# Expert pairs of a hybrid decoder step: the pair's combine moved into the next pair's first layer, the gather one pair ahead, the decode rows' results in four column groups, the last norm tile by tile

## The chip, the cores and the metric

One core of a Trainium2 chip. The metric is the device time of one execution in microseconds, lower is better. Engines: PE is TensorE (PEld its weight loads), DVE VectorE, ACT ScalarE, POOL GpSimd, SP SyncE, which issues most DMAs. All times of the trace count from the start of the span.

## The reference, cut to what matters

One layer of a decoder step for 264 tokens of width 1024: 256 prompt rows and 8 decode rows. A mixer (gated short convolution and retention, merged by gates) gives `h`. Then a mixture of 32 experts adds to it, each token going to its best 4, and a last RMS norm closes:

```
def expert_ffn(xb, w1, b1, w2, b2):
    h = xb @ w1 + b1
    gate, up = h[:, :D_FF], h[:, D_FF:]
    gate = jnp.minimum(gate, 7.0)
    up = jnp.clip(up, -7.0, 7.0)
    return ((up + 1.0) * gate * jax.nn.sigmoid(1.702 * gate)) @ w2 + b2

h = h + sum over the token's 4 experts e of gate[e] * expert_ffn(rmsnorm(h, norm2), e)
y = rmsnorm(h, norm_f)          # y_prompt: 256 rows, y_sample: 8 rows
```

All weights are float32; `w1` is 1024 x 2048 and `w2` 1024 x 1024 per expert, 12.6 MB an expert, 403 MB for all 32.

## The kernel before, in words

The first 530 us are the mixer, the router and the splitting of the normed rows into three bf16 parts (`xp`, `xps`). They don't change, apart from the width of `rg`. Then comes the expert loop: 16 pairs of experts, in as many rounds as the fullest expert needs slots (64 slots an expert; one round here).

**Weights.** `load_pair` (line 522) runs on SP. The ring is used as six wide slots of 2.097 MB. A pair is 12 transfers: four for each first layer (two k of 128 rows each), two for each second layer (four f each). Transfer n waits until PE has used the contents of its slot (`used`, lines 507 to 520, by the semaphores `chunk_used`, `up_done`, `down_done`) and is issued at line 534. PE waits for a slot in `slot_ready` (line 1504).

**One pair on PE, in order** (lines 1516 to 1590): the gather (1518 to 1526), 64 bf16 products of the row parts with the one-hot matrix `P`, into banks 6 and 7; the first layer of expert 0 (1530 to 1547), which begins with a bias product (1542) and writes banks 0 and 1; three transposes of the weighted one-hots `Pg` into bank 5 (1552 to 1555); the first layer of expert 1 into banks 2 and 3; then for each expert four transposes of its activation into bank 5 (1563), a bias product (1570) and the second layer (1572 to 1581), both experts into bank 4; then the combine (1585 to 1590): for each of three row tiles (128, 128 and 8 rows) and two column halves, a product of the turned `Pg` with the results `ysb`, into bank 6 or 7, so from the third product on each waits for an add.

**The other engines in a pair.** POOL copies the two experts' columns of `rg` (644) and the row picker `pick` for the bias products (646). DVE builds `P` and `Pg` (1204, 1206), copies the high half of the gathered rows (1208), clips and multiplies the activations (1212 to 1220), copies the low half of the results (1223) and adds the six combined pieces to `hx` (1227). ACT copies the low half of the gathered rows (853), the turned `Pg` (855), takes the sigmoids (859), copies the turned activations (862) and the high half of the results (864). The next pair's `P` is built after the last add, in DVE's order, and the next gather waits for it and for the adds (1516, 1517).

**The end** (866 to 875, 1231 to 1238, 547 to 553): ACT squares each of the three tiles with a sum per row; DVE turns the three sums into means at once, ACT takes the roots, DVE the reciprocals; then DVE scales the two prompt tiles, which SP stores, and POOL and ACT scale the decode rows.

**Start of the loop.** ACT copies the last prompt states out of PSUM (842) and issues their stores (844); POOL forms the last remainders (633). Both are ahead of the loop in their engines' orders. Each float32 product is two PE instructions in the trace.

## Time and profile before

| | |
|---|---|
| median of 3 runs | 1487.25 us (1486.15 to 1487.38) |
| the profiled execution's own time | 1487.55 us |
| its span | 1485.8 us, 17919 instructions |
| busy | PE 93%, PEld 48%, DVE 25%, ACT 15%, POOL 6% |
| chain that ended last | PE 84%, DMA 7%, DVE 4%, ACT 3% |
| read from HBM | 496 MB |

How to read it: the chain is followed back from the last instruction, at each step to what released it. A window gives, for a stretch of time, how long each engine was busy, the clock that PE was granted (1.00 is 2.4 GHz) and the DMA engines' mean busy share, which can come out slightly over 1. Ends of matmuls are modelled, so a busy PE need not be at its peak.

### The profile page before, as it was taken

Reading aid. Unit: us, or ns where it says so; the run is one execution under the profiler, and the core shown is the slowest. Engines: PE = TensorE matmul, PEld = TensorE weight load, DVE = VectorE, ACT = ScalarE, POOL = GpSimd, SP = SyncE. Lnnn points to the kernel's source line nnn. Section 1 sums busy time; section 2 is a strip of 40 time slices with the busy share of each in tenths; the row PEclk is TensorE's granted clock in tenths of the full one; section 3 lists DMA queues with packets and bytes.
Section 4 is the critical chain, followed back from the end, with each engine's and each line's share of the span. In section 5 each row is a group of like instructions: output and inputs, shape, how many; then the busy total and the mean of one; then the engine's idle time right before and its main releaser. Section 6 shows DMA issues by size and latency. Waiting matters only on the chain.

```text
span 1485.8 us, 17919 instructions
## 1 busy us (share of the span) xinstructions
PE 1382.9 (93%) x7365; PEld 707.5 (48%) x7365; DVE 374.4 (25%) x677; ACT 228.7 (15%) x340; POOL 96.2 (6%) x160
## 2 busy tenths in 40 slices
PE   8999989999999988998999989989999899899996
PEld 7667658778888533332433333324333333233331
DVE  3224332532411332122121221221212212211123
ACT  1122222211000421111101111111011111110102
POOL 1122222210000210000000000000000000000000
PEclk9999999999999999999999999999999999999999
DMA  9788867875243469999999999999999999999993
GB/s 373 293 290 277 289 215 281 291 270 208 114 156 135 180 274 428 412 421 431 414 423 430 412 430 422 428 429 421 425 430 427 428 419 421 430 428 418 430 422 136
DMA packets 52063, 518.48 MB, mean 349 GB/s; under 512 B 6167, under 2 KB 6439, under 8 KB 19742
## 3 DMA queue, kind: packets, MB, share of 16 engines
q1 hardware_dynamic: 37370, 469.09, 75.9%
q0 software_dynamic: 12720, 45.14, 9.0%
q10 hardware_dynamic: 1940, 3.78, 0.7%
q8 instruction: 25, 0.41, 0.1%
q14 instruction: 8, 0.07, 0.0%
HBM read 496.35 MB, written 21.67 MB: 349 GB/s over the span
## 4 chain that ended last, share of the span: by engine, by line
PE 84%; DMA 7%; DVE 4%; ACT 3%; issue 1%; POOL 0%; DVEq 0%; SPq 0%; POOLq 0%; ACTq 0%
PE bank L1544 30%; PE bank L1272 17%; PE bank L1578 15%; PE bank L1589 6%; DMA out_ret_sample<-arena 5%; PE bank L1523 4%; PE bank L1315 3%; PE bank L1409 2%; PE bank L1542 1%; ACT arena L862 1%; PE bank L1570 1%; DMA k_kept<-arena 1%; DVE arena L1212 1%; DVE arena L1223 1%; DVE hx L1227 1%
## 5 line engine op out<-in xcount | busy, mean ns | idle before, releaser
L1544 PE MATMUL bank<-ring,arena 128*64 128x512 f32 x2048 | 444.8, 592 | 0.0
L1272 PE MATMUL bank<-arena,ring 128*128 128x264 f32 x1536 | 350.5, 388 | 0.0
L1272 PEld LDWEIGHTS bank<-arena,ring 128*128 128x128 f32 x1536 | 290.3, 190 | 53.5 <-issue 5.0
L1544 PEld LDWEIGHTS bank<-ring,arena 128*64 128x64 f32 x2048 | 143.7, 137 | 283.0 <-issue 277.3
L1578 PE MATMUL bank<-ring,arena 128*64 128x512 f32 x1024 | 225.1, 592 | 0.0
L1578 PEld LDWEIGHTS bank<-ring,arena 128*64 128x64 f32 x1024 | 71.8, 137 | 131.9 <-issue 129.4
L1212 DVE TENSOR_SCALAR arena<-bank 128x512 f32<-128x512 f32 x32 | 22.1, 692 | 396.5 <-PE bank L1544 396.5
L1589 PE MATMUL bank<-arena 128*128 128x512 f32 (+1 forms) x192 | 91.3, 610 | 12.6 <-DVE arena L1223 12.6
L1523 PE MATMUL bank<-arena 128*128 128x128 bf16 x768 | 61.6, 240 | 31.3 <-DVE arena L1204 31.3
L1223 DVE COPY arena<-bank 64x512 f32<-64x512 f32 x32 | 21.9, 683 | 229.0 <-PE bank L1578 229.0
L1523 PEld LDWEIGHTS bank<-arena 128*128 128x128 bf16 x768 | 56.1, 109 | 46.0 <-issue 46.0
L1227 DVE TENSOR_TENSOR hx<-hx,bank 128x512 f32<-128x512 f32 (+1 forms) x96 | 65.6, 683 | 38.0 <-PE bank L1589 38.0
L1589 PEld LDWEIGHTS bank<-arena 128*128 128x128 f32 (+1 forms) x192 | 23.6, 155 | 79.5 <-DVE hx L1227 45.1
L1315 PE MATMUL bank<-ring,arena 128*128 128x512 f32 x128 | 57.8, 605 | 0.0
L864 ACT ACTIVATE arena<-bank 64x512 f32<-64x512 f32 x32 | 19.0, 593 | 236.0 <-PE bank L1578 236.0
L646 POOL CAST arena<-cst 128x128 bf16 x16 | 4.7, 293 | 764.0 <-DVE arena L1223 764.0
L859 ACT ACTIVATE arena<-arena 128x512 f32<-128x512 f32 x32 | 20.1, 629 | 203.3 <-DVE arena L1212 203.1
L855 ACT ACTIVATE arena<-bank 128x264 f32<-128x264 f32 x16 | 6.3, 391 | 258.6 <-PE bank L1553 258.6
L1570 PE MATMUL bank<-arena 128*64 128x512 bf16 x64 | 13.0, 403 | 33.4 <-ACT arena L862 33.4
L973 DVE SCALAR_TENSOR_TENSOR arena<-arena 128x512 f32<-128x512 f32 x32 | 24.0, 750 | 78.5 <-ACT arena L686 63.1
L686 ACT ACTIVATE arena<-arena 128x1024 f32<-128x1024 f32 x32 | 33.6, 1050 | 48.7 <-DMA arena<-in_state_ret 48.2
L1315 PEld LDWEIGHTS bank<-ring,arena 128*128 128x128 f32 x128 | 24.2, 194 | 28.2 <-issue 28.2
(198 smaller groups left out, 817.7 us busy)
## 6 DMA issues: line engine op xcount, KB each, us to landing
ring<-in_w_pairs SPq DMA_DIRECT2D x192, 2048.0 KB, 15.2
ring<-in_w_mixer SPq DMA_DIRECT2D x60, 1024.0 KB, 9.1
arena<-in_state_ret POOLq DMA_DIRECT2D x32, 512.0 KB, 6.9
out_ret_sample<-arena POOLq DMA_DIRECT2D x32, 512.0 KB, 6.4
arena<-v_decode POOLq DMA_DIRECT2D x32, 256.0 KB, 8.3
out_ret_prompt<-arena ACTq DMA_DIRECT2D x4, 512.0 KB, 5.3
hx<-in_x_prompt SPq DMA_DIRECT2D x2, 512.0 KB, 3.8
v_kept<-arena ACTq DMA_DIRECT2D x2, 512.0 KB, 9.4
```

Source lines behind the costliest of these rows:

```text
L686: ac.activation(S[n % 3], S[n % 3], ACT.Copy, scale=gamma(n // NS)).then_inc(S_scaled, 1)
L1212: v.tensor_scalar(gcl[:, e, :], psum[2 * e][:, :], LIMIT, None, ALU.min).then_inc(g_clip, 1)
L1223: v.tensor_copy(ysb[SLOTS * e:SLOTS * (e + 1), 0:512], psum[4][0:64, :]).then_inc(y_ready, 1)
L1227: v.tensor_tensor(hx[0:n, t, 512 * c:512 * (c + 1)], hx[0:n, t, 512 * c:512 * (c + 1)], psum[6 + c][0:n, :], ALU.add).then_inc(added, 1)
L1272: ins = pe.matmul(bank[:, 0:T], weight(n + k // 4, k % 4)[:, 128 * j:128 * (j + 1)], rhs[:, k, :], start=k == 0, stop=k == KD * groups - 1)
L1315: ins = pe.matmul(bank[:, :], xnT[:, k, 128 * t:128 * (t + 1)], w, start=k == 0, stop=k == KD - 1)
L1409: ins = pe.matmul(bank[:, :], merged[:, k, 128 * t:128 * (t + 1)], weight(n + 2 * c + k // 4, k % 4), start=k == 0, stop=k == KD - 1)
L1523: pe.matmul(out, xp[:, t, part, 128 * k:128 * (k + 1)], P[:, 2 * t:2 * t + 2, :], start=t == 0 and part == 0, stop=False)
L1544: ins = pe.matmul(out, xgT[:, k, 64 * e:64 * (e + 1)], held(n, 2 * D * (k % W1_KS) + c), start=False, stop=k == KD - 1)
L1570: pe.matmul(psum[4][64 * half:64 * (half + 1), :], pick[:, e, :], bp2[:, 512 * half:512 * (half + 1)], start=True, stop=False)
L1578: ins = pe.matmul(psum[4][64 * half:64 * (half + 1), :], lhs, held(n, D * (f % W2_FS) + 512 * half), start=False, stop=f == KD - 1)
L1589: pe.matmul(psum[6 + c][0:n, :], pgT[:, 128 * t:128 * t + n], ysb[:, 512 * c:512 * (c + 1)], start=True, stop=True).then_inc(combined, 1)
```

## The change

In the expert loop the combine of pair n moves into the first layer of expert 0 of pair n+1, between its sixth and seventh k; pair 0 combines zeros, and one more combine follows the last pair. The gather of pair n+1 moves to the place between pair n's second first layer and its transposes; there are 17 gathers a round, the last on two columns of zeros that `rg` gains. The decode rows' results get a tile of their own, `hs`, with 4 groups of 32 partitions by 256 columns: their combine is four products of 32 columns by 256, in one bank, and one add. Every combined piece has a bank of its own, the two experts' transposes use banks 5 and 3 and their results banks 4 and 2. The last norm runs by tile and half: for each half a square with its sum on ACT, the mean carried into the second half's sum by a bias. The decode rows' sum over groups is a product with a 0/1 matrix (`tail`, loaded by POOL). POOL and ACT scale prompt tile 0 and ACT stores it; DVE scales tile 1 and the decode rows. The diff, cut:

```diff
-ADDED = 5
+ADDS = 5
+ADD_BANKS = (3, 6, 7, 4, 2)
+TURN_BANKS = (5, 3)
+Y_BANKS = (4, 2)
...
-                    sp.dma_start(o["y_sample"][:, 0, :], y_last[0:NS, :]).then_inc(y_out, 16)
-            sp.wait_ge(y_out, 16 * TT)
+            sp.wait_ge(hs_out, 1)
+            for j in range(4):
+                sp.dma_start(o["y_sample"][:, 0, 256 * j:256 * (j + 1)], hs[32 * j:32 * j + NS, :]).then_inc(y_out, 16)
+            for c in range(2):
+                sp.wait_ge(y_scaled, c + 1)
+                sp.dma_start(o["y_prompt"][0, 128:256, 512 * c:512 * (c + 1)], hx[:, 1, 512 * c:512 * (c + 1)]).then_inc(y_out, 16)
+            sp.wait_ge(y_out, 16 * 7)
...
 
+            was_filled(pool, ("wo", 1, 1))
+            pool.dma_start(arena[:, 7456:7456 + 384], a["tail"]).then_inc(tail_in, 16)
+            pool.memset(pgT[:, :], 0.0).then_inc(pad_zero, 1)
...
+            def columns(g, it, e):
+
+                pool.wait_ge(P_ready, 2 * g + PRIMED)
+                pool.tensor_copy(rgc[:, :, :, :], rg[:, :, :, bass.ds(e, 2)]).then_inc(cols_ready, 1)
+                pool.wait_ge(pick_read, it + PRIMED)
+                pool.tensor_copy(pick[:, :, :],
+                                 cst[:, bass.ds(e + C_PICK, 2)].rearrange("p (e o) -> p e o", o=1)
+                                 .to_broadcast([128, 2, SLOTS])).then_inc(pick_ready, 1)
...
 
-            pool.wait_ge(added, 6 * PAIRS * rounds + ADDED)
-            pool.tensor_tensor(y_last[0:NS, :], hx[0:NS, 2, :], nfb[0:NS, :], ALU.mult).then_inc(gained, 1)
+            for c in range(2):
+                pool.wait_ge(added, ADDS * PAIRS * rounds + (c + 2))
+                pool.tensor_tensor(y_first[:, 512 * c:512 * (c + 1)], hx[:, 0, 512 * c:512 * (c + 1)],
+                                   nfb[:, 512 * c:512 * (c + 1)], ALU.mult).then_inc(gained, 1)
...
+            ac.wait_ge(hs_zero, 1)
+            for j in range(4):
+                ac.activation(hs[32 * j:32 * j + NS, :], hx[0:NS, 2, 256 * j:256 * (j + 1)], ACT.Copy).then_inc(hs_ready, 1)
...
             with ac.Fori(0, rounds) as r:
+                low_half(r * GATHERS)
                 with ac.Fori(0, PAIRS) as pair:
                     it = r * PAIRS + pair
...
                     ac.wait_ge(pg_turned, it + (1 + PRIMED))
-                    ac.activation(pgT[:, :], psum[5][:, 0:T], ACT.Copy).then_inc(pgT_ready, 1)
+                    ac.wait_ge(pad_zero, 2)
+                    ac.activation(pgT[:, 0:T], psum[TURN_BANKS[0]][:, 0:T], ACT.Copy).then_inc(pgT_ready, 1)
                     for e in range(2):
                         ac.wait_ge(g_clip, 2 * it + e + 1)
                         ac.wait_ge(st_out, 16 * H)
                         ac.activation(sig[:, e, :], gcl[:, e, :], ACT.Sigmoid, scale=ALPHA).then_inc(sig_ready, 1)
+                    low_half(r * GATHERS + pair + 1)
                     for e in range(2):
                         ac.wait_ge(act_turned, 2 * it + e + 1)
-                        ac.activation(actT[:, e, :], psum[5][:, :], ACT.Copy).then_inc(actT_ready, 1)
+                        ac.activation(actT[:, e, :], psum[TURN_BANKS[e]][:, :], ACT.Copy).then_inc(actT_ready, 1)
+                    for e in range(2):
                         ac.wait_ge(down_done, 2 * it + e + 1)
-                        ac.activation(ysb[SLOTS * e:SLOTS * (e + 1), 512:1024], psum[4][64:128, :], ACT.Copy).then_inc(y_hi_ready, 1)
+                        ac.activation(ysb[SLOTS * e:SLOTS * (e + 1), 512:1024], psum[Y_BANKS[e]][64:128, :], ACT.Copy)\
+                            .then_inc(y_hi_ready, 1)
...
+            ac.wait_ge(added, ADDS * PAIRS * rounds + 1)
+            ac.activation(squares3[:, 4, 0:256], hs[:, :], ACT.Square, accum_out=stat[:, 4:5]).then_inc(hs_squared, 1)
+            for n, (t, c) in enumerate(ADD_TILES):
+                ac.wait_ge(added, ADDS * PAIRS * rounds + (n + 2))
+                ac.activation(squares3[:, n, :], hx[:, t, 512 * c:512 * (c + 1)], ACT.Square,
+                              accum_out=stat[:, n:n + 1]).then_inc(half_squared, 1)
+                ac.wait_ge(half_squared, n + 1)
+                if c == 0:
+                    ac.activation(stat[:, 5 + t:6 + t], stat[:, n:n + 1], ACT.Identity, scale=1.0 / D,
+                                  bias=stat[:, 15:16]).then_inc(mean3, 1)
+                    ac.wait_ge(mean3, t + 1)
+                else:
+                    ac.activation(stat[:, 8 + t:9 + t], stat[:, n:n + 1], ACT.Sqrt, scale=1.0 / D,
+                                  bias=stat[:, 5 + t:6 + t]).then_inc(root3, 1)
+                if n == 1:
+                    ac.wait_ge(hs_summed, 1)
+                    ac.activation(stat[:, 7:8], psum[3][:, 0:1], ACT.Sqrt, scale=1.0 / D, bias=stat[:, 15:16]).then_inc(hs_root, 1)
             ac.wait_ge(inv3, 1)
-            ac.wait_ge(gained, 1)
-            ac.activation(y_last[0:NS, :], y_last[0:NS, :], ACT.Copy, scale=stat[0:NS, 11:12]).then_inc(y_last_ready, 1)
+            for c in range(2):
+                ac.wait_ge(gained, c + 1)
+                ac.activation(y_first[:, 512 * c:512 * (c + 1)], y_first[:, 512 * c:512 * (c + 1)], ACT.Copy,
+                              scale=stat[:, 10:11]).then_inc(y_first_ready, 1)
+            ac.wait_ge(y_first_ready, 2)
...
+            def add_results(n):
+
+                v.wait_ge(combined, ADDS * n + 1)
+                v.tensor_tensor(hs[:, :], hs[:, :], psum[ADD_BANKS[0]][:, 0:256], ALU.add).then_inc(added, 1)
+                for i, (t, c) in enumerate(ADD_TILES):
+                    v.wait_ge(combined, ADDS * n + (i + 2))
+                    v.tensor_tensor(hx[:, t, 512 * c:512 * (c + 1)], hx[:, t, 512 * c:512 * (c + 1)],
+                                    psum[ADD_BANKS[i + 1]][:, :], ALU.add).then_inc(added, 1)
+                v.wait_ge(added, ADDS * n + ADDS)
...
             with v.Fori(0, rounds) as r:
+                one_hots(r * GATHERS, r * PAIRS)
+                high_half(r * GATHERS)
                 with v.Fori(0, PAIRS) as pair:
...
+                    add_results(it)
+                    activate(it, 0)
+                    one_hots(r * GATHERS + pair + 1, it + 1)
+                    activate(it, 1)
+                    high_half(r * GATHERS + pair + 1)
                     for e in range(2):
                         v.wait_ge(down_done, 2 * it + e + 1)
-                        v.tensor_copy(ysb[SLOTS * e:SLOTS * (e + 1), 0:512], psum[4][0:64, :]).then_inc(y_ready, 1)
-                    for t, n in enumerate(ROWS):
-                        for c in range(2):
-                            v.wait_ge(combined, 6 * it + 2 * t + c + 1)
-                            v.tensor_tensor(hx[0:n, t, 512 * c:512 * (c + 1)], hx[0:n, t, 512 * c:512 * (c + 1)],
-                                            psum[6 + c][0:n, :], ALU.add).then_inc(added, 1)
...
+            v.wait_ge(tail_in, 16)
+            v.wait_ge(hs_root, 1)
+            v.reciprocal(stat[:, 14:15], stat[:, 7:8]).then_inc(hs_inv, 1)
+            v.wait_ge(hs_inv, 1)
+            v.scalar_tensor_tensor(hs[:, :], hs[:, :], stat[:, 14:15], nfs, ALU.mult, ALU.mult).then_inc(hs_out, 1)
             for t in range(2):
-                v.scalar_tensor_tensor(hx[:, t, :], hx[:, t, :], stat[:, 9 + t:10 + t], nfb[:, :],
-                                       ALU.mult, ALU.mult).then_inc(y_scaled, 1)
+                v.wait_ge(root3, t + 1)
+                v.reciprocal(stat[:, 10 + t:11 + t], stat[:, 8 + t:9 + t]).then_inc(inv3, 1)
+            v.wait_ge(inv3, 2)
+            for c in range(2):
+                v.scalar_tensor_tensor(hx[:, 1, 512 * c:512 * (c + 1)], hx[:, 1, 512 * c:512 * (c + 1)], stat[:, 11:12],
+                                       nfb[:, 512 * c:512 * (c + 1)], ALU.mult, ALU.mult).then_inc(y_scaled, 1)
 
...
+            def combine(n):
+
+                pe.wait_ge(y_ready, 2 * n + PRIMED)
+                pe.wait_ge(y_hi_ready, 2 * n + PRIMED)
+                pe.wait_ge(actT_ready, 2 * n + PRIMED)
+                for j in range(4):
+                    ins = pe.matmul(psum[ADD_BANKS[0]][32 * j:32 * (j + 1), 0:256], pgT[:, LP:LP + 32],
+                                    ysb[:, 256 * j:256 * (j + 1)], start=True, stop=True)
+                ins.then_inc(combined, 1)
+                for i, (t, c) in enumerate(ADD_TILES):
+                    pe.matmul(psum[ADD_BANKS[i + 1]][:, :], pgT[:, 128 * t:128 * (t + 1)], ysb[:, 512 * c:512 * (c + 1)],
+                              start=True, stop=True).then_inc(combined, 1)
+
             with pe.Fori(0, rounds) as r:
+                gather(r * GATHERS)
...
+                    pe.wait_ge(pick_ready, g + 1)
+                    first_layer(0, range(-1, 6))
+                    combine(it)
+                    first_layer(0, range(6, KD))
...
+                    pe.wait_ge(added, ADDS * it + ADDS)
+                    first_layer(1, range(-1, KD))
+                    gather(g + 1)
+
+                    pe.wait_ge(pgT_ready, it + 1)
                     for e in range(2):
-
                         pe.wait_ge(act_ready, 2 * it + e + 1)
...
+                            ins = pe.transpose(psum[TURN_BANKS[e]][:, 128 * k:128 * (k + 1)], acts[:, e, 128 * k:128 * (k + 1)], ident)
                         ins.then_inc(act_turned, 1)
+                    for e in range(2):
+                        for half in range(2):
+                            ins = pe.matmul(psum[Y_BANKS[e]][64 * half:64 * (half + 1), :], pick[:, e, :],
+                                            bp2[:, 512 * half:512 * (half + 1)], start=True, stop=False)
+                        if e == 1:
+                            ins.then_inc(pick_read, 1)
...
+            pe.wait_ge(xg_hi, GATHERS * rounds + PRIMED)
+            combine(PAIRS * rounds)
+            pe.wait_ge(hs_squared, 1)
+            pe.wait_ge(tail_in, 16)
+            pe.matmul(psum[3][:, 0:1], same_row, stat[:, 4:5], start=True, stop=True).then_inc(hs_summed, 1)
```

## Rows read from the trace of the kernel before

**Rows 1.** Windows: length, busy PE, PEld, DVE, ACT, POOL, PEclk, DMA share, GB/s

```profile
540.00:1440.00 900.00, 827.35 (x4298) 307.00 (x4296) 191.89 (x289) 108.49 (x153) 7.41 (x30) 0.99 1.00 424
590.00:600.00 10.00, 10.00 (x72) 5.12 (x71) 0.69 (x1) 0.60 (x1) 0.00 (x0) 0.92 0.89 352
...
602.00:652.00 50.00, 1.00 1.01 430
1378.00:1424.00 46.00, 1.00 1.01 430
```

**Rows 2.** Chain of waits, pairs from 587.84 and 648.13: start, length, engine, line

```profile
587.84 0.59 PE bank L1523 x6
...
648.13 0.51 PE bank L1523 x6
...
651.98 13.73 PE bank L1544 x64
...
666.79 13.76 PE bank L1544 x64
...
682.47 0.41 PE bank L1570 x2
682.87 6.89 PE bank L1578 x32
...
698.38 0.70 DVE arena L1223
699.12 5.72 PE bank L1589 x12
...
706.79 0.51 PE bank L1523 x6
```

**Rows 3.** Line 534 alone: issue at 536.5, then the last issue at 1444.5

```profile
L534 SPq DMA_DIRECT2D ring<-in_w_pairs x1: 328/328/328, 536.5 to 536.5; - x1
...
DMA to landing us min/median/max: 7.8/7.8/7.8
...
L534 SPq DMA_DIRECT2D ring<-in_w_pairs x1: 333/333/333, 1444.5 to 1444.5; - x1
...
DMA to landing us min/median/max: 15.4/15.4/15.4
```

**Rows 4.** Chain, decode rows' output product; timeline, four transposes of an activation

```profile
479.84 2.59 PE bank L1456 x48
...
740.74 0.66 PE L1564 MATMUL bank<-cst,arena 128*128 128x128 f32 x4
```

**Rows 5.** Timeline at the loop's start; line 808 (min/median/max ns)

```profile
528.00 0.41 ACTq L844 DMA_DIRECT2D out_ret_prompt<-arena  x1
...
528.40 0.62 DVE L1204 TENSOR_TENSOR arena<-cst,rgc 128x384 bf16<-128x384 f32 x1 [1.10 <-POOL rgc L644]
...
L808 ACT ACTIVATE arena<-bank x4: 373/375/378, 482.5 to 483.7; 8x256 f32<-8x256 f32 x4
```

**Rows 6.** Windows, columns as in rows 1: a wait for activation, a combine's end

```profile
681.00:684.40 3.40, 2.05 (x12) 0.73 (x12) 2.25 (x4) 1.11 (x2) 0.00 (x0) 1.00 0.98 419
705.00:708.00 3.00, 1.21 (x19) 1.22 (x20) 1.65 (x3) 0.00 (x0) 0.19 (x1) 0.93 1.03 437
```

**Rows 7.** The end: chain, timeline, and two groups of the page (busy, mean ns)

```profile
1469.82 5.72 PE bank L1589 x12
...
1469.69 1.28 ACT L866 ACT_TABLE_LOAD   x1
...
1476.31 2.33 POOL L657 TENSOR_TENSOR arena<-hx,arena 8x1024 f32<-8x1024 f32 x1 [64.44 <-DVE hx L1227]
...
1481.67 0.36 SPq L549 DMA_DIRECT2D out_y_prompt<-hx  x1
...
L1227 DVE TENSOR_TENSOR hx<-hx,bank 128x512 f32<-128x512 f32 (+1 forms) x96 | 65.6, 683 | 38.0 <-PE bank L1589 38.0
L859 ACT ACTIVATE arena<-arena 128x512 f32<-128x512 f32 x32 | 20.1, 629 | 203.3 <-DVE arena L1212 203.1
```

More of the change, by code:

```diff
@@ L38 @@
 MAX_ROUNDS = -(-T // SLOTS)
+GATHERS = PAIRS + 1
 ALPHA = 1.702
@@ L155, in laid_out_experts, with laid_out_tail @@
     return out
+def laid_out_tail(inputs):
+    p = np.arange(128)
+    same_row = (p[:, None] % 32 == p[None, :] % 32).astype(np.float32)
+    return np.concatenate([same_row, np.repeat(inputs["norm_f"].reshape(4, 256), 32, axis=0)], axis=1)
 PROJ_BANKS = 3
@@ L651, in _ @@
+            with pool.Fori(0, rounds) as r:
+                with pool.Fori(0, GATHERS) as pair:
+                    columns(r * GATHERS + pair, r * PAIRS + pair, 2 * pair)
+                pool.wait_ge(cols_ready, GATHERS * (r + 1))
                 pool.tensor_tensor(rg[:, 0, :, :], rg[:, 0, :, :],
-                                   cst[:, C_THR + 1:C_THR + 2].rearrange("p (a o) -> p a o", a=1).to_broadcast([128, TT, E]),
+                                   cst[:, C_THR + 1:C_THR + 2].rearrange("p (a o) -> p a o", a=1).to_broadcast([128, TT, E + 2]),
@@ L881, in _ @@
             steps = [0]
-            for primed in (P_ready, y_ready):
+            for primed in (P_ready, y_ready, xg_hi):
                 v.sem_inc(primed, PRIMED)
-            v.sem_inc(added, ADDED)
             def own(ins):
@@ L1605 @@
     arrays["tables"] = shape_constants()
+    arrays["tail"] = laid_out_tail(inputs)
     arrays["w_mixer"] = laid_out_mixer(inputs)
```

181 lines of the change are left out of this document (77 added, 104 removed).

## The prediction

> **What bounds the kernel now.** I read the windows first, then the chain of waits of one pair of experts, the DMA issues, the start of the expert loop and the end. The windows show two resources used up at once: from 540 to 1440 us the DMA engines have a share of 1.00 and move 424 GB/s, and PE is busy for 827 of 900 us [rows 1]. The chain decides between them. In the pair that starts at 648.13 every link is PE, or the DVE and ACT steps that PE waits for; no link is a transfer. The next pair starts at 706.79, 58.66 us later [rows 2]. A pair takes 12 transfers of 2.097 MB. Between dips the rate is 430 GB/s; over 14 such stretches of 46 to 50 us, of which the first and the last stand in the rows, it lies between 428 and 431, mean 429.3 [rows 1]. So a transfer costs 2.097/0.4293 = 4.885 us and a pair's data 58.6 us. PE and data are level, with PE a hair behind: once a pair, after the long stretch in which PE frees no slot (698.35 to about 715: combine, adds, gather, first two k), all six wide slots are full and the DMA engines dry up, as at 590 to 600 (share 0.89, 352 GB/s) [rows 1]. The issues say it over the whole loop: the first transfer into a freed slot is issued at 536.5 and lands 7.8 later, at 544.3; the last is issued at 1444.5 and lands at 1459.9 [rows 3]. That is 185 landings in 915.6 us, 4.949 each, where 4.885 is possible. And PE ends its last product at 1469.1, 9 us after the data are there: it is PE that is late.
>
> **The change on PE, per pair.** What stays: gather, both first layers with their bias products and the turn of Pg, 648.13 to 680.55 = 32.42 us; twice 0.41 + 6.89 for the second layers = 14.60 [rows 2]. Two sets of four transposes now stand free in PE's order: the row has 0.66 for four, partly overlapped, I take 0.6 each, 1.2 [rows 4]. Combine: 4 products of 128x512 instead of 6; 5.72 for six with their waits is 0.95 each [rows 2], 3.8, an upper bound, since no product waits for an add any more (each has a bank of its own). The decode rows: eight instructions of 256 columns in four column groups; the nearest row is L1456, the same form, 48 in 2.59, so 0.43 [rows 4]. Sum 32.42 + 14.60 + 1.2 + 4.2 = **52.4 us** against 58.66.
> What goes is waits: 680.55 to 682.47 for the first activation (1.92), 1.29 between the experts (698.35 less 689.76 less a bias product and a second layer), 0.77 for the last copy of the results, the add between combine products, and 706.79 - 704.84 = 1.95 from the last product over the add and the new one-hots to the next gather [rows 2]. Is each truly covered? The first layer of the second expert (13.8) hides activation, one-hots and column copies of the first; gather ahead and the first transposes (3.3 + 0.6) hide the second activation (four DVE steps of 0.7, 2.8, [rows 7] for the width); the second transposes and a bias product (1.0) hide the 0.6 copy of the first. The adds run on DVE under the last two k of expert 0 (3.4 us); PE then waits for all five before it writes banks 2 and 3, and the fifth ends 0.7 after the combine. DVE's order puts activation 0 behind the adds: they are over before it is due. POOL's column and pick copies wait for earlier events than before. If these covers failed the price would be the old waits, 6 us a pair, and no more.
>
> **What is late next: the data.** With PE at 52.4 and data at 58.6, PE gains 6.2 a pair on a lead of six slots (29 us), so after four or five pairs it waits for transfers, in pieces of at most 4.885 - 3.43 = 1.45 us a chunk (a chunk is a quarter of 13.73 [rows 2]). The longest stretch without a freed slot falls from 17 us to about 9, under two transfers, so the ring no longer stands full and the dips go: 185 x (4.949 - 4.885) = 12 us. In the first pair, the zero combine (4.2) stretches one release; three transfers (14.7) are in flight over it, so no dip. The 17th gather of the last pair lies in the data wait; uncovered it would cost 3.3.
>
> **The start.** DVE's first one-hots ran at 528.40, when POOL's columns were there. Now DVE waits until ACT has copied the four decode groups, and these stand behind ACT's last issue, 528.00 + 0.41. Four copies of 8x256 at 0.375 = 1.5 [rows 5], and 0.2 for DVE to enter its loop (an estimate: 0.1 to 0.4): 1.7 us later. POOL's new issue and two memsets end in 1.2 to 2.5; I take 1.7, range 1.5 to 3. All of it counts, since the first slot comes free that much later: first landing at 546.0.
>
> **The end.** Last landing 546.0 + 185 x 4.885 = 1449.7. PE works its last chunk (3.45) and DVE copies (0.75): combine starts at 1453.9. Before, from that point (1469.82) to the last output issue (1481.67) went 11.85, and 4.1 more to the end of the span [rows 7]. Now ACT is the longest line: free after its table load (1469.69 + 1.28, and a dummy root) at +1.4, a square of 256 columns (0.5), four squares of 512 (0.63 + 0.19 for reading the sum), a small step of 0.2 after each, one root for the decode rows, 0.5 of hand-overs: +6.8. Then DVE's reciprocal 0.2, two halves of 0.7, and the last issue at +8.5. Gone are the mean of all three tiles on DVE, the square of 1024 columns behind the last add, and the two adds of 8 rows (0.68 each) [rows 7]. SP has four small issues for the decode rows (1.4) that end at about +7, before the first half is ready. After the last issue as much data is left as before (a quarter of the prompt's rows there, half on ACT's queue), 4.1 to 4.6: +12.8 in all. Uncertain is POOL, which multiplies tile 0's halves while DVE adds tile 1: POOL's row has 2.33 for 1024 columns, 1.17 a half [rows 7]; held up fully, an add costs from nothing to 1.2. I take nothing, as the first half of it lies in ACT's shadow.
> The Trainium skill (GPSIMD Engine Reference, Key points) says that the two engines contend where a DVE instruction has two SBUF inputs; the adds have one and a PSUM bank, so by the page too nothing is added; no row here shows the pair.
>
> **Sum.** 1449.7 + 3.45 + 0.75 + 12.8 = 1466.7 of span, against 1485.8. The profiled execution was 1487.55, 1.75 over its span, and 0.3 over the median of 1487.25: 1468.5.
>
> **Rivals.**
> 1. The dips stay (they are the DMA's own, not the full ring). For: the share reads 1.00 even in slow stretches. Against: they come once a pair, after the stretch without a release, and a transfer issued there lands as fast as the lone one. Then 185 x 4.949: last landing 1461.6, time **1480**. Chance 0.12.
> 2. The clock: slower. PE will now idle in most chunks of the loop's later part. In the trace the granted clock is 1.00 (2.4 GHz) through the activation wait at 681 to 684.4, PE busy 2.05 of 3.4; at 705 to 708, PE busy 1.21 of 3.0, it begins to fall to 1.2 GHz [rows 6]. Such a fall cost 1.6 us a pair (60.29 from 587.84 to 648.13, against 58.66 [rows 2]). A data wait of 1.45 in 4.9 leaves PE as busy as the first of these, so I expect none. If each wait brought a fall, five a pair would make 52.4 + 8 = 60.4, and from gather 0 (528.40 + 0.76 + 1.7) 530.9 + 16 x 60.4 + 13.6 = 1511 of span, time **1513**. The point at which it turns against the kernel is four falls a pair (58.8). Up to three are free, in the slack of 6.2. Chance 0.06.
> The Trainium skill (TensorE: Matmul & The Clock Gate, HAM oscillation) speaks for this rival: it describes a kernel whose data waits between short bursts put PE back to the half clock at every tile. Its waits were longer than its bursts; here it is the other way round.
> 3. The order doesn't do what it says: a wait of about 6 us a pair appears in the new places (the one-hots behind activation 0, or `added` ahead of the second expert). PE stays at 58.7 and only the tail gains, or loses the start: **1485 to 1489**, no change. Against: each cover above has 1 us or more to spare. Chance 0.04.
>
> **Numbers.** Forecast 1468.5 with chance 0.78; its own range 1463 to 1475 (rate 428 to 431: 3 either way; start and tail 2 each; a fallen clock in the last chunk and combine, up to 5, upwards only). The range reaches to rival 1: 1462 to 1481. A measurement of this kernel tells 0.2% (3 us) from no change. Faster 0.90, same 0.04, slower 0.06.
>
> **What would show it.** In the profile after: transfers in the chain from the fifth pair on; 12 landings every 58.6 us, no stretch under 420 GB/s after the first pairs; PE busy about 52 us a pair; last landing near 1450; the adds under the first expert's last products; the tail from last product to end 13.5 instead of 16.7. Wrong if the chain is PE throughout, if the rate dips once a pair, or if the clock shows many slices under 9.

## The result, and the profile after

The changed kernel takes **1474.38 us** (median of 4 runs, 1472.07 to 1475.95), the kernel before 1487.32 beside it (4 runs, 1486.15 to 1488.13): a ratio of 0.9912, 95% interval 0.9895 to 0.993. That is 12.9 us less, where the forecast was 18.8 less than its median. The time lies in the forecast's range of 1462 to 1481, and only 0.6 inside the narrower one of 1463 to 1475. The profiled execution took 1473.57, its span is 1471.8.

First lines of the page of the changed kernel: the granted clock and the rate in 40 slices, the chain by engine, and the costliest group of the loop (busy, mean ns, idle before and what ended it).

```profile
PEclk9999999999999999999999999999999999999999
...
GB/s 371 299 296 271 292 227 296 278 274 192 134 157 115 177 208 426 429 429 428 427 428 428 429 428 430 428 427 428 428 429 428 430 428 427 429 427 429 428 430 228
...
DMA 53%; PE 43%; issue 1%; DVE 1%; ACT 1%; POOL 0%; SPq 0%; ACTq 0%; DVEq 0%; POOLq 0%
...
L1644 PE MATMUL bank<-ring,arena 128*64 128x512 f32 x2048 | 461.0, 596 | 62.8 <-DMA ring<-in_w_pairs 61.3
```

From the sixteenth slice on the rate is 426 to 430 GB/s in every slice but the last. The chain was 84% PE before; now it is 53% DMA. PE stood idle 61.3 us ahead of the first layers' products because a transfer had not landed. The chain shows where that sets in. It is given from the end of pair 0 to the first two waits for data; columns are start, length, line and count.

```profile
573.67 7.00 PE bank L1683 x32
...
580.89 6.87 PE bank L1683 x32
...
588.19 10.30 PE bank L1644 x48
598.49 0.57 PE bank L1604 x8
599.06 3.63 PE bank L1608 x8
...
625.53 7.00 PE bank L1683 x32
...
647.09 24.02 DMA ring<-in_w_pairs
...
671.16 3.68 PE bank L1644 x16
```

The second layers run back to back (573.67, 580.89) with no step of ACT or DVE between them, and the next first layer follows at once. The combine, four products of 512 columns in 3.63 with the decode rows' eight in 0.57, has no wait for an add in it. From second layer to second layer (573.67 to 625.53) a pair is 51.86 us; the forecast had 52.4, and the row before 58.66 [rows 2]. At 647.09 the link is a transfer, 24.02 from issue to landing, in the third pair. The clock stays: this is the window of the loop from 562 on, columns as in [rows 1].

```profile
562.00:1440.00 878.00, 804.50 (x4371) 299.91 (x4368) 175.63 (x273) 106.92 (x151) 7.36 (x30) 1.00 1.01 429
```

The end, as links of the chain:

```profile
1429.85 24.32 DMA ring<-in_w_pairs
...
1454.21 3.68 PE bank L1683 x16
...
1457.91 0.69 DVE arena L1305
...
1458.65 0.64 PE bank L1604 x8
```

The last data land at 1454.2, PE works them off in 3.68, and the final combine begins right behind DVE's copy of the results. PE is no longer late: from the last landing to that copy it is 3.8 us, where it was 9.2.

The next table sets the kernels by the same six events (us of each profile; "count" is DVE's write of the round count, the last routing step common to all; landings are issue plus time to landing, both to a tenth; "step" is the mean distance of the 185 landings behind the first, in e8 and e9 of 371 half-size ones taken twice, in e12 of 92 double-size ones taken half).

| | count | first one-hots | first refill issued | lands | last landing | step | copy of results | end of span |
|---|---|---|---|---|---|---|---|---|
| before | 526.4 | 528.4 | 536.5 | 544.3 | 1459.9 | 4.949 | 1469.1 | 1485.8 |
| changed | 524.5 | 530.1 | 539.8 | 547.7 | 1454.1 | 4.899 | 1457.9 | 1471.8 |
| changed again (r0) | 526.9 | 531.1 | 541.9 | 549.8 | 1456.2 | 4.899 | 1460.0 | 1473.8 |
| e1 half the data | 525.2 | 529.3 | 540.0 | 545.2 | 1345.8 | | 1365.9 | 1379.7 |
| e2 combine twice | 531.2 | 536.8 | 547.2 | 555.0 | 1466.6 | 4.928 | 1470.9 | 1488.2 |
| e3 before, short gather | 528.7 | 530.7 | 539.3 | 547.1 | 1453.5 | 4.899 | 1457.3 | 1474.0 |
| e4 copies early | 530.1 | 532.9 | 542.7 | 550.3 | 1456.9 | 4.901 | 1460.7 | 1474.5 |
| e5 combine ahead | 528.2 | 534.0 | 549.9 | 557.6 | 1464.5 | 4.902 | 1468.2 | 1482.0 |
| e6 gather behind | 526.8 | 533.7 | 543.4 | 551.2 | 1457.8 | 4.901 | 1461.6 | 1478.8 |
| e7 old order | 525.0 | 533.9 | 542.1 | 549.9 | 1456.4 | 4.900 | 1460.1 | 1480.8 |
| e8 half-size transfers | 522.9 | 528.8 | 537.9 | 542.6 | 1467.5 | 4.986 | 1469.5 | 1482.7 |
| e9 start mended, half-size | 523.8 | 526.0 | 532.7 | 537.7 | 1461.3 | 4.979 | 1463.3 | 1476.5 |
| e10 start mended | 524.7 | 526.9 | 536.3 | 544.2 | 1450.7 | 4.900 | 1454.5 | 1468.3 |
| e12 double-size transfers | 526.6 | 532.4 | 546.3 | 558.5 | 1455.1 | 4.87 | 1462.3 | 1475.5 |

The count itself moves from 523 to 531 between profiles although no kernel changes the routing that leads to it, so the start is read from it on. Before to changed, in spans: start +5.3 (17.9 to 23.2), 185 landings -9.2 (915.6 to 906.4), last landing to copy -5.4, tail -2.8 (16.7 to 13.9), mixer -1.9 by that chance; together -14.0.

### The profile page after: what moved, and what is told of

Read it like the earlier page. It is cut to its first block, busy times and chain, and to the rows that moved or that the text cites. A ratio compares the mean times of both kernels' runs of the same rounds, so it can differ in the third digit from the quotient of the medians.

```text
span 1471.8 us, 18292 instructions
## 1 busy us (share of the span) xinstructions
PE 1367.5 (93%) x7503; PEld 705.3 (48%) x7503; DVE 362.3 (25%) x671; ACT 233.6 (16%) x355; POOL 99.5 (7%) x167
## 4 chain that ended last, share of the span: by engine, by line
DMA 53%; PE 43%; issue 1%; DVE 1%; ACT 1%; POOL 0%; SPq 0%; ACTq 0%; DVEq 0%; POOLq 0%
DMA ring<-in_w_pairs 46%; PE bank L1353 18%; PE bank L1644 11%; DMA out_ret_sample<-arena 5%; PE bank L1396 3%; PE bank L1683 2%; PE bank L1490 2%; PE bank L1593 1%; PE bank L1608 1%; PE bank L1455 1%; DMA k_kept<-arena 1%; PE bank L1444 0%; POOL arena L595 0%; DMA arena<-v_decode 0%; PE bank L1433 0%
## 5 line engine op out<-in xcount | busy, mean ns | idle before, releaser
L1644 PE MATMUL bank<-ring,arena 128*64 128x512 f32 x2048 | 461.0, 596 | 62.8 <-DMA ring<-in_w_pairs 61.3
L1644 PEld LDWEIGHTS bank<-ring,arena 128*64 128x64 f32 x2048 | 141.4, 137 | 364.5 <-issue 273.3
L1683 PE MATMUL bank<-ring,arena 128*64 128x512 f32 x1024 | 229.0, 595 | 11.5 <-DMA ring<-in_w_pairs 11.5
L1683 PEld LDWEIGHTS bank<-ring,arena 128*64 128x64 f32 x1024 | 70.9, 137 | 153.3 <-issue 124.9
L1608 PE MATMUL bank<-arena 128*128 128x512 f32 x136 | 62.9, 605 | 0.0
L1273 DVE TENSOR_TENSOR hs<-hs,bank 128x256 f32<-128x256 f32 x17 | 7.2, 421 | 223.7 <-PE bank L1604 223.7
L1593 PEld LDWEIGHTS bank<-arena 128*128 128x128 bf16 x816 | 51.9, 99 | 17.8 <-issue 17.8
L1593 PE MATMUL bank<-arena 128*128 128x128 bf16 x816 | 56.7, 222 | 4.0 <-DVE arena L1260 4.0
L1276 DVE TENSOR_TENSOR hx<-hx,bank 128x512 f32<-128x512 f32 x68 | 46.8, 688 | 19.0 <-PE bank L1608 19.0
L1608 PEld LDWEIGHTS bank<-arena 128*128 128x128 f32 x136 | 24.4, 189 | 31.4 <-issue 31.4
```

The lines of the kernel that those rows point to most:

```text
L1276: v.tensor_tensor(hx[:, t, 512 * c:512 * (c + 1)], hx[:, t, 512 * c:512 * (c + 1)], psum[ADD_BANKS[i + 1]][:, :], ALU.add).then_inc(added, 1)
L1593: pe.matmul(out, xp[:, t, part, 128 * k:128 * (k + 1)], P[:, 2 * t:2 * t + 2, :], start=t == 0 and part == 0, stop=False)
L1608: pe.matmul(psum[ADD_BANKS[i + 1]][:, :], pgT[:, 128 * t:128 * (t + 1)], ysb[:, 512 * c:512 * (c + 1)], start=True, stop=True).then_inc(co ...
L1644: ins = pe.matmul(out, xgT[:, k, 64 * e:64 * (e + 1)], held(n, 2 * D * (k % W1_KS) + c), start=False, stop=k == KD - 1)
L1683: ins = pe.matmul(psum[Y_BANKS[e]][64 * half:64 * (half + 1), :], lhs, held(n, D * (f % W2_FS) + 512 * half), start=False, stop=f == KD - 1)
```

## The experiments

The theory: data bound the loop once PE is shorter than 58.8 us a pair, and what is missing was lost at the start. The rivals: PE still has a part in the bound (e1, e2, e3), the order matters more than its length (e5, e6, e7), the lost microseconds lie in the rate of the transfers (e8, e12). Ratios are to the kernel before on the same chip, whose medians were 1486.65 (e1 to e4), 1487.63 (r0, e7 to e9) and 1490.26 (e5, e6, e10, e12).

**Half the data (e1).** Every wide transfer moves half of its columns.

```diff
-                    dst = ring[:, at:at + SLOT_CHUNKS, :].rearrange("p a n -> p (a n)")
-                    src = w_pairs[bass.ds(pair, 1), n].rearrange("o p n -> p (o n)")
+                    dst = ring[:, at:at + SLOT_CHUNKS, :].rearrange("p a n -> p (a n)")[:, 0:WIDE // 2]
+                    src = w_pairs[bass.ds(pair, 1), n].rearrange("o p n -> p (o n)")[:, 0:WIDE // 2]
```

> The changed kernel, with each of the 192 expert transfers cut to the first half of its slot (1.05 MB instead of 2.1); PE does all its work, half of it on what the slot held before, so the experts' results are not the reference's. Theory (the loop is bound by the transfers, PE needs 51.9 us a pair): no link of the loop's chain is a transfer, a pair takes 51.9 us, and the time falls by (58.8 - 51.9) us a pair from the point where PE had caught up, to about 1381 us. Rival (PE's new waits are the bound, data only look late): the pair stays near 58.7 and the time near 1474.

One run: 1381.56 us. The window of the loop and the combine of two pairs in the chain:

```profile
560.00:1340.00 780.00, 780.00 (x4317) 300.84 (x4315) 173.96 (x270) 106.25 (x150) 7.29 (x30) 1.00 0.73 243
```

```profile
702.39 0.57 PE bank L1604 x8
...
754.25 0.57 PE bank L1604 x8
```

PE is busy for all of 780 us and a pair is 51.86 again. So this is PE's own length, and the changed kernel waits 6.9 us a pair for data. As expected, no link of the loop's chain is a transfer. The time is 92.8 us below the changed kernel's median: about the most that shorter transfers could bring to this order.

**More work on PE (e2).** Each pair's four combine products of the prompt tiles run twice.

```diff
                 ins.then_inc(combined, 1)
+                for i, (t, c) in enumerate(ADD_TILES):
+                    pe.matmul(psum[ADD_BANKS[i + 1]][:, :], pgT[:, 128 * t:128 * (t + 1)], ysb[:, 512 * c:512 * (c + 1)],
+                              start=True, stop=True)
                 for i, (t, c) in enumerate(ADD_TILES):
```

> The changed kernel, with the four prompt products of each combine done twice (3.6 us more of PE a pair, same result). Theory: the pair has 6.7 us of slack on PE, so nothing changes but the last combine, which stands bare: 1474 + 4 = 1478 us at most, and the loop's landings stay 4.90 us apart. Rival (PE bound): 16 x 3.6 = 58 us more, 1532.

1483.04 (1480.17 to 1490.05, 10 runs), ratio 0.9972 [0.9961, 0.9984], some 9 us more than the changed kernel. A pair is 55.3, well under 58.8, and the windows (length, clock, share, GB/s) show a steady stream and one hole:

```profile
564.00:568.00 4.00, 1.00 0.45 111
600.00:1400.00 800.00, 1.00 1.01 429
```

The hole is in the first pair. There the products, 3.43 long from 558.23, stand ahead of the next release, nothing is left in flight, and the DMA engines run dry: from 564 to 566 us they move nothing. Over the stream that is 185 x (4.928 - 4.899) = 5.4, and nothing gives it back, since every later transfer is already at full rate. The end is longer too, 17.3 instead of 13.9, since the last combine is also doubled. So "slack of 6.9 a pair" is only had once the data are behind.

**Less work on PE in the kernel before (e3).** Its gather uses one of the three bf16 parts of the rows.

```diff
-                                for part in range(3):
+                                for part in range(1):
```

> The kernel before, with the gather's second and third bf16 parts left out (32 of 56 products; 1.9 us less of PE a pair; the gathered rows lack their lower bits). Theory (the kernel before was bound by PE by a hair, and the once-a-pair dips of the transfer rate come from a full ring): PE needs 56.8 a pair, the dips go after the first pairs, landings come every 4.89 instead of 4.949, last landing near 1449, and the end as in the kernel before behind it (last products 3.5, then 16.7): 1471 to 1474 us. Rival (the dips are the DMA's own): landings stay at 4.949 and the last at 1460; 1483.

1476.28 (4 runs), ratio 0.993 [0.9911, 0.9949]. This is the old order with its old waits, and the loop's window reads

```profile
600.00:1400.00 800.00, 729.23 (x3450) 249.02 (x3447) 170.69 (x257) 98.06 (x139) 6.91 (x28) 0.99 1.01 428
```

with the same step, 4.899, as the changed kernel, and the same 3.8 from the last landing to the copy. What made the dips was that PE was slower than the data over the whole loop (4.949 x 12 = 59.4 a pair), so that the ring stood full once a pair. Here PE's own pair is 56.9 (from 705.71 to 762.58, between the adds that two gathers wait for). A PE a little faster than 58.8 a pair gets the whole gain of the stream; whatever else the change takes off PE in the loop is worth nothing here. The tail stays the old one, 16.7.

**The order turned back, both at once and singly (e7, e6, e5).** e7: all of combine, adds and gather stand between the pairs again, everything else as changed; the combine of zeros and its adds stand ahead of the first gather. e6: only the gather goes behind the second layers. e5: only the combine goes ahead of the first layer.

```diff
# e5
-                    first_layer(0, range(-1, 6))
+                    pe.wait_ge(xg_lo, g + (1 + PRIMED))
+                    pe.wait_ge(xg_hi, g + (1 + PRIMED))
                     combine(it)
-                    first_layer(0, range(6, KD))
+                    first_layer(0, range(-1, KD))
```

```diff
# e7, on PE (e6 moves gather(g + 1) alone)
-                    combine(it)
...
-                    gather(g + 1)
...
+                    combine(it + 1)
+                    pe.wait_ge(added, ADDS * it + 2 * ADDS)
+                    gather(g + 1)
```

The copies of the gathered rows (`low_half`, `high_half`) move along on ACT and DVE, and in e7 the adds.

> The changed kernel with the order of the kernel before: combine behind the second layers of its own pair, adds behind it, then the gather; the decode rows' groups, a bank for every piece, the turned banks and the new end stay. Theory (any 1 to 2 us a pair taken from PE makes the transfers the bound; the turn of the loop is more than is needed): PE needs 56 to 57 a pair, landings stay at 4.90, and only the start moves, by the zeros' combine ahead of gather 0, 1 to 2 us: 1475 to 1477. Rival (the turned order is what gives the gain): the pair goes back to 58.7 to 59.3 on PE, the last product ends 7 to 9 us behind the last landing, 1482 to 1487.

> The changed kernel with the next pair's gather moved behind the second layers (combine inside the first layer as in the changed kernel), so the activation's wait stands bare again. Theory: PE needs 54 to 55 a pair, landings stay at 4.90; the 17th gather and its copies now stand between the last second layer and the last combine, 3 to 4 us: 1478. Rival (gather ahead is what gives the gain): landings at 4.94 or more, 1483 or more.

> The changed kernel with the whole combine put ahead of the first layer of expert 0 instead of into it; gather one pair ahead as in the changed kernel. Theory: PE needs 52.7 a pair, far under 58.8, so landings stay at 4.90 and the end is the same; only in pair 0 the zeros' combine now stands ahead of the first freed slot, so the first landing is 4.2 to 4.9 us later: 1479 to 1480. Rival (where the combine stands matters in every pair): 0.77 us and the adds a pair, 16 times, 1487 or more.

e7: 1483.29, 0.9969 [0.9958, 0.998]. e6: 1480.23, 0.9911 [0.9879, 0.9944]. e5: 1483.83, 0.9952 [0.9933, 0.997]. By its time alone e6 isn't told from the changed kernel. None loses in the stream: the steps are 4.900, 4.901 and 4.902. In e7 the chain of a pair early in the loop is PE and the DVE steps that it waits for, with no transfer, and takes 57.96 from one gather to the next; from 1183 us on, when PE has caught up, transfers are in the chain:

```profile
650.67 0.49 PE bank L1593 x6
...
708.63 0.49 PE bank L1593 x6
```

Of these 57.96, 1.7 is the clock: behind the bare wait for the activation the first of the two second layers takes 8.56 at a granted clock of 0.80, the other 6.89 at 1.00. What the three lose in their spans lies at the two ends. In e7 the tail is 20.7 instead of 13.9. Its timeline (start, length, engine, line, idle before):

```profile
1465.19 0.69 DVE L1276 TENSOR_TENSOR hx<-hx,bank 128x512 f32<-128x512 f32 x1 [0.17 <-PE bank L1608]
...
1466.16 0.49 PE L1593 MATMUL bank<-arena 128*128 128x128 bf16 x6 [1.01 <-DVE hx L1276]
...
1467.92 0.60 ACT L886 ACTIVATE arena<-bank 128x512 f32<-128x512 f32 x1 [7.19 <-PE bank L1595]
...
1468.54 1.28 ACT L908 ACT_TABLE_LOAD   x1
...
1469.49 0.69 DVE L1268 COPY arena<-bank 128x512 f32<-128x512 f32 x1 [3.61 <-PE bank L1595]
1469.83 0.20 ACT L908 ACTIVATE stat<-stat 128x1 f32<-128x1 f32 x1
```

The gather of a pair that doesn't exist follows the last add, ACT's copy of it stands ahead of its table load and squares, DVE's copy ahead of the norm: ACT begins the last norm at 1469.83 although the first half of the first tile was added up at 1463.3 (the first add begins at 1462.61 and takes 0.69). In e6 the same gather stands ahead of the combine (tail 17.2). In e5 the tail is the changed kernel's, 13.8, but from the one-hots to the first refill it is 15.9 where it was 9.8. Its timeline at the start:

```profile
541.62 0.64 PE L1604 MATMUL bank<-arena 128*32 128x256 f32 x8 [1.17 <-DVE arena L1268]
...
545.93 0.69 DVE L1276 TENSOR_TENSOR hx<-hx,bank 128x512 f32<-128x512 f32 x1 [0.17 <-PE bank L1608]
...
549.92 0.33 SPq L552 DMA_DIRECT2D ring<-in_w_pairs  x1
```

The combine of zeros stands ahead of the first release. So of the 8.3 us between e7 and r0 on one chip (1483.29 and 1475.01) 6.9 lie in the tail (20.7 and 13.8), 2.0 in the start (24.9 and 22.9 from the count to the first landing), and none in the middle; the count came 1.9 earlier in e7's profile.

**The start (e4, e10).** e4 moves ACT's four copies of the decode rows ahead of its two state copies. e10 also moves POOL's new issue and two fills ahead of its last splits.

```diff
# ACT (e4, e10): from behind the last state's store to behind the copies of xps
+            ac.wait_ge(hs_zero, 1)
+            for j in range(4):
+                ac.activation(hs[32 * j:32 * j + NS, :], hx[0:NS, 2, 256 * j:256 * (j + 1)], ACT.Copy).then_inc(hs_ready, 1)
...
# POOL (e10 alone): from behind the splits to ahead of the fifth
+                if i == 4:
+                    was_filled(pool, ("wo", 1, 1))
+                    pool.dma_start(arena[:, 7456:7456 + 384], a["tail"]).then_inc(tail_in, 16)
+                    pool.memset(pgT[:, :], 0.0).then_inc(pad_zero, 1)
+                    pool.memset(ysb[:, :], 0.0).then_inc(pad_zero, 1)
```

> The changed kernel, with ACT's four copies of the decode rows into their groups moved from just ahead of the loop to a point where ACT idles (behind the copies into xps). Theory: DVE's first one-hots start when POOL's columns are there, 527.2 instead of 530.1 in the trace of the changed kernel, PE idles less and its clock does not fall in gather 0 (1.3 us), all of which moves the first landing and the end: 3 to 4 us less than the changed kernel, near 1471. Rival (POOL's two memsets and its load are as late, or the start does not reach the end): under 1 us less.

> The changed kernel with the decode rows' copies early and POOL's load and memsets ahead of its last four subtractions; slots of 2.1 MB as in the changed kernel. Theory (start and stream add up): 18 to 19 us from the count of rounds to the first landing instead of 23, landings 4.90 apart, the end unchanged: 4 to 5 us less than the changed kernel, 1470. Rival (what the start wins is lost in the stream): 1474 to 1475.

e4: 1473.61 (6 runs, 1467.18 to 1476.35), 0.9898 [0.9877, 0.9919], by its time alone not told from the changed kernel. e10: **1470.48** (4 runs, 1469.69 to 1471.78), 0.9859 [0.9838, 0.988], below the changed kernel's 0.9912 and 0.992 (r0); the intervals of e10 and of the first comparison don't touch. The start of the changed kernel's loop, to be read against [rows 5]:

```profile
524.50 0.15 DVE L1234 CAST rounds_i<-arena 128x1 int32<-128x1 f32 x1
...
524.57 1.27 DVE L1235 TENSOR_SCALAR rg<-arena 8x32 f32<-8x32 f32 x1
...
524.84 0.97 POOL L658 MEMSET arena<- 128x1024 f32 x1
...
526.90 0.60 ACT L871 ACTIVATE arena<-bank 128x512 f32<-128x512 f32 x1 [1.49 <-PE bank L1526]
...
527.53 0.41 ACTq L873 DMA_DIRECT2D out_ret_prompt<-arena  x1
527.99 1.73 ACT L878 ACTIVATE hs<-hx 8x256 f32<-8x256 f32 x4 [0.48 <-ACT arena L871]
...
530.06 0.56 DVE L1260 TENSOR_TENSOR arena<-cst,rgc 128x384 bf16<-128x384 f32 x1 [3.71 <-ACT hs L878]
...
530.87 0.49 PE L1593 MATMUL bank<-arena 128*128 128x128 bf16 x6 [4.00 <-DVE arena L1260]
...
539.81 0.33 SPq L552 DMA_DIRECT2D ring<-in_w_pairs  x1
```

Here DVE is ready at 526.3 and builds the one-hots at 530.06, behind ACT's copy at 526.90, its store's issue and the copies (1.73 for four). PE waits 4.00. Three DVE steps, of which the first is shown, take 1.27, 1.12 and 0.99 and end together at 525.84, 0.03 after POOL's second fill; before they were 0.22, 0.20 and 0.17. And this is what the clock did in those stretches:

```profile
526.90:530.90 4.00, 0.03 (x1) 0.07 (x2) 0.71 (x2) 3.42 (x6) 0.49 (x2) 1.00 0.35 131
530.90:535.80 4.90, 4.90 (x58) 4.72 (x60) 0.41 (x1) 2.00 (x3) 0.20 (x1) 0.65 0.01 3
```

It fell during the gather. The same stretch of e10:

```profile
524.71 0.15 DVE L1233 CAST rounds_i<-arena 128x1 int32<-128x1 f32 x1
524.78 0.22 DVE L1234 TENSOR_SCALAR rg<-arena 8x32 f32<-8x32 f32 x1
...
526.86 0.64 DVE L1259 TENSOR_TENSOR arena<-cst,rgc 128x384 bf16<-128x384 f32 x1 [1.22 <-POOL rgc L667]
...
528.19 0.83 PE L1592 MATMUL bank<-arena 128*128 128x128 bf16 x6
...
536.25 0.33 SPq L552 DMA_DIRECT2D ring<-in_w_pairs  x1
```

The one-hots stand 2.15 behind the count (5.56 in the changed kernel), and the gather takes 3.6 instead of 4.8. In e4, where only the copies moved, the DVE step beside the fill still takes 1.26 and the one-hots stand 2.8 behind. In all, from count to first landing: changed 23.2, r0 22.8, e4 20.2, e10 19.5, before 17.9.

**Size of the transfers (e8, e9, e12).** The constant that sets a slot's chunks goes from 4 to 8 (twelve slots of 1.05 MB) and to 2 (three of 4.19 MB); e9 is e8 with the start of e10.

```diff
-W1_CHUNKS = 4
+W1_CHUNKS = 8
```

> The changed kernel with the expert weights in 12 slots of 1.05 MB instead of 6 of 2.1 (24 transfers a pair; same bytes, same PE work). Theory (the loop is a stream of transfers that starts when PE frees its first slot and after which only PE's last chunk and the end remain): the first slot is free 1.72 us earlier and PE's work behind the last landing falls from 3.65 to 1.8: 3.5 us less than the changed kernel, 1471. Rival 1 (smaller transfers are slower): landings over 2.45 us apart, each 0.01 us costs 3.8 us. Rival 2 (PE bound): no change.

> The changed kernel with three edits: the early copies of the decode rows and the 12 slots, both as in their own runs, and POOL's load and two memsets moved ahead of its last four subtractions, where it idles. Theory: the start costs 17 to 18 us from the count of rounds to the first landing less 1.7 for the half slot, against 23 in the changed kernel (DVE's last routing steps no longer take 1.0 to 1.3 us each beside the memsets, where they took 0.2); with the end's 1.8 the sum is 7 to 9 us less than the changed kernel: 1466. Rival (the start's gain is lost in the stream of transfers): as the run with 12 slots alone, 1471.

> The changed kernel with the expert weights in 3 slots of 4.2 MB (6 transfers a pair, rows of 32 KB a partition). Theory (a packet is a partition's row of a transfer: 16 KB take 613 ns and 8 KB 312 ns in the traces, so about 11 ns a packet and 301 ns for each 8 KB): a 32 KB row takes 1.215 us, 2.1 MB take 4.86 instead of 4.90, 8 us less over the loop; against it the first slot is free 3.4 later and the last chunk is 3.4 longer, and the ring dries for 1 to 2 us in pair 0: 1474 to 1477. Rival (rows are cut at 16 KB anyway, so no faster stream): 1482 to 1485.

e8: 1484.84 (12 runs), 0.9986 [0.9971, 1.0001], nearly all of the change's gain lost. e9: 1481.27 (9 runs), 0.9963 [0.9949, 0.9976]. e12: 1476.34, 0.9894 [0.9871, 0.9918], as the changed kernel. The smaller transfers did what was hoped at both ends (first landing 4.7 after its issue instead of 7.9, the copy 2.0 after the last landing instead of 3.8) and lost 185 x (4.986 - 4.899) = 16 us in between, in e9 15. It isn't the issues that come late: in e8 SP's issue takes 1.9 us in the median (0.33 in the changed kernel), but the DMA engines' share is 1.01 from 600 to 1400 us, at 422 GB/s. The larger transfers of e12 win 5 us in the stream (184 x (4.899 - 4.87)) and pay for it at both ends: 31.9 from the count to the first landing, and the copy 7.2 behind the last. One hundred microseconds of the loop by packets, first the changed kernel, then e8, then e12 (packets, bytes, rate):

```profile
DMA packets 2941, 42.91 MB, mean 429 GB/s; under 512 B 322, under 2 KB 322, under 8 KB 322
```

```profile
DMA packets 5793, 42.20 MB, mean 422 GB/s; under 512 B 642, under 2 KB 642, under 8 KB 642
```

```profile
DMA packets 1481, 43.25 MB, mean 433 GB/s; under 512 B 161, under 2 KB 161, under 8 KB 161
```

Without those under 512 B that is 2619, 5151 and 1320 packets, each a row of one partition of 16.4, 8.2 and 32.8 KB. With 16 engines busy all 100 us one takes 1600/2619 = 0.611 us, 0.311 and 1.212: half the bytes take more than half the time. That the step follows the row's length is argued from these three sizes; each of them changes the length of a transfer as well.

**The changed kernel again (r0).** The same file, beside e7 to e9.

> The changed kernel itself, unaltered, as the base for the kernels beside it on the same chip. Theory: 1474 us within the 2 us that the mixer's own length moves it, landings 4.90 us apart, and some 23 us from the count of rounds on DVE to the first landing of the loop. No rival.

1475.01 (6 runs, 1470.14 to 1481.59), 0.992 [0.9895, 0.9944]. From the first landing on its stages agree with the first profile within 0.1 us. From the count to that landing it takes 22.8 (23.2 there), but the parts differ. Links of its chain:

```profile
525.10 2.79 PE bank L1526 x6
...
531.87 0.80 PE bank L1593 x6
...
537.82 0.55 PE bank L1642 x4
```

The last state products (L1526) run at full clock, the one-hots stand 4.15 behind the count (5.56 there), and the gather takes 5.9 (4.8 there) at a granted clock of 0.52. PE's idle time ahead of the gather is 4.00 in both.

## Why the prediction was right, and where it was off

**The bound, the dips and rival 1: right.** The reading that PE was late, and that the dips were a full ring, holds: they are gone, and e3 takes them away in the kernel before by shortening PE alone. The term was sized 185 x (4.949 - 4.885) = 12; it is 9.2, since the step is 4.899. The rate taken was the mean of stretches between dips, 429.3; over the loop it is 428.1 (2.097/4.899). That is 0.3% of 906 us, 2.7 us, the second largest error. The forecast's own range (428 to 431) held it.

**PE's sum: right.** 51.86 against 52.4, the covers hold; what is late next is the data, from the third pair on instead of the fifth. The prediction gave PE a lead of six slots, 29 us; but the first refill lands 11.5 us after PE begins with the first slot (536.2 to 547.7). Six slots are half a pair of PE's work, 25.9, so the lead is 14.4 (an estimate), which 6.9 a pair use up in two pairs. What the prediction did not say is that most of this gain is of no use: e3, e6 and e7 reach the same stream.

**Rival 2, the clock: rightly held unlikely in the loop.** PE works a chunk off in 3.7 (671.16) of each 4.9 and waits for data in between, and the clock is 1.00 from 562 to 1440 us. The Trainium skill (TensorE: Matmul & The Clock Gate, HAM oscillation) describes a kernel whose clock falls at every data wait, with waits longer than the bursts between them; the trace here shows no fall, with PE busy for the longer part of each 4.9. The clock did cost something where the prediction had not looked: at the start.

**The start: the step that failed.** It was priced at 1.7, range 1.5 to 3, and measured 5.3 (4.9 in r0). The copies themselves were sized nearly right: the prediction had four of 0.375 and 0.2 of hand-over, and they took 1.73 and 0.34. What failed is that their length was taken for the whole term, and that the clock of the products around the new wait was put at nothing. Two parts are in both profiles of the changed kernel. PE stands idle 4.00 us between its last state products and the gather, where it was 1.83: 2.2. And the gather behind this wait is slower: 4.8 at a granted clock of 0.65, in r0 5.9 at 0.52, where it took 3.2 at 1.00: 1.6 and 2.7. In e9, where PE waits only 0.4, it takes 3.2 again. A third part is in the first profile alone. ACT's last state copy waits for PE's last state products, so the store and the copies behind it come later when these are slow:

```profile
524.49 2.84 PE L1445 MATMUL bank<-arena 128*128 128x512 f32 x6
```

```profile
522.71 4.16 PE L1526 MATMUL bank<-arena 128*128 128x512 f32 x6
```

The first line is of the profile before, the second of the one after, where the granted clock is 0.68 over these products: the store came 3.03 after the count instead of 1.63, and 1.3 of the 5.3 is this; with the 2.2 and the 1.6 that is 5.1. It belongs to the execution and not to the change: r0 has 2.84 too, and e3, whose order is the old one, has 4.51 and yet a start of 18.4, since there no one-hots wait behind ACT. So a new wait behind a queue was priced with the queue, and the clock, as one profile had them. With the copies early and POOL's work out of the way the term is +1.6 (e10). That this is near the forecast's 1.7 is luck: no copy is waited for in e10, but its state products took 5.49 at 0.50, and the gather follows them directly (528.19).

**From the last landing, and the tail: right.** The forecast was 4.2 to the combine's start (measured 4.5) and 12.8 from there (13.2, 1458.65 to 1471.8); together -8.85 forecast, -8.2 measured. POOL's multiplications did not hold up DVE's adds:

```profile
1461.15 2.50 POOL L685 TENSOR_TENSOR arena<-hx,arena 128x512 f32<-128x512 f32 x2 [10.38 <-DVE hx L1276]
1461.24 0.69 DVE L1276 TENSOR_TENSOR hx<-hx,bank 128x512 f32<-128x512 f32 x1 [0.17 <-PE bank L1608]
```

The add that starts 0.09 behind POOL takes 0.69, as the one alone. The Trainium skill (GPSIMD Engine Reference, Key points) names contention where DVE's instruction has two SBUF inputs or runs in a two-port mode; the trace agrees, with 0.69 for one SBUF and one PSUM input.

**The sum.** Forecast -19.1 of span, measured -14.0: start 3.6 too little, stream 2.7, last landing and tail 0.6, and 1.9 the other way from a mixer that happened to end early. That last is luck: without it the profiled 1473.57 would be 1475.5, just over the narrow range's upper end, where r0's median of 1475.01 also lies. The forecast also names the 0.3 by which the profiled execution lay above the median, and doesn't take it off. Rival 3's new waits did come, but at the start alone, not once a pair.

## What to carry to other kernels

When two resources are nearly level, the gain of a faster PE ends where it passes the data (here at 58.8 us a pair, from 59.4), and one short cut that gets there is worth as much in the loop as a turned order. While the transfers are the bound, everything ahead of the first released slot counts in full and is never given back, so whatever a new order puts there (copies behind another engine's late work, fills beside DVE's short steps) belongs earlier. A stream that is the bound runs faster with long rows, as long as the ends don't take it back (they did in e12), and slack measured in its steady state is no slack in its first pair.

## What the runs showed of the hardware that was not expected

- Packets of 8, 16 and 32 KB give 422, 429 and 433 GB/s with the DMA engines busy throughout, though every transfer's own latency (24 us in the loop) is hidden. The Trainium skill (SBUF — State Buffer, The DMA setup-cost knee) names 436 GB/s as the limit that ever larger transfers approach; the trace agrees, with 433 for the largest.
- Three DVE steps of 0.2 took 1.0 to 1.3 and ended with POOL's fill of 128x1024. With the fills moved they took 0.22, 0.20 and 0.17. That the first waited and held up the others is argued from their common end.
- The six last state products follow PE's 2.3 us of idleness in the router. They took 2.84 in four of the fourteen profiles (before, r0, e1, e4), 4.16 to 4.54 in eight and 5.49 in two (e6, e10); the granted clock over them was 1.00 (before, r0), 0.68 (changed) and 0.50 (e6, e10). The same wait can cost 0 or 2.6 us.
